# Column sums of squares taken tile by tile on TensorE in two norms beside the first attention

## What is computed

```python
def rms_norm(x, g):
    xf = x.astype(jnp.float32)
    y = xf * lax.rsqrt(jnp.mean(xf * xf, axis=-1, keepdims=True) + EPS)
    return (y * g.astype(jnp.float32)).astype(x.dtype)

a = spatial_gating_unit(jax.nn.gelu(u), jax.nn.gelu(v), ...)      # 512 tokens x 512
b = nsa_attention(q, kv, gl, ...)                                 # the first attention
mixed = jnp.concatenate([rms_norm(a, mix_out_g[l, 0]), rms_norm(b, mix_out_g[l, 1])], axis=-1)
x = x + mixed @ w_out[l]
...
k, v = jnp.split(rms_norm(mem, kv_norm_g) @ w_mkv, 2, axis=-1)    # 256 tokens x 1024
```

## Time and profile before

| | |
|---|---|
| median of 3 runs | 2616.11 us (2615.8 to 2616.41) |
| the profiled execution, its own time | 2613.08 us |
| its span, first to last instruction | 2611.3 us |
| mean granted clock of PE | 0.968 of 2.4 GHz |
| PE busy | 2467.3 us, 94% of the span |
| POOL busy | 532.1 us, 20% |
| the loop of the first attention | about 208 to 376 us |

### The profile page before, as it was taken

How to read it: one execution, slowest core, us unless ns; L and a number is a source line. 1 busy time by engine, 2 the same in 40 slices (tenths; PEclk the granted TensorE clock), 3 DMA queues, 4 the chain that set the end, 5 groups by cost and what they waited for, 6 DMA issues and landing times.

```text
span 2611.3 us, 34190 instructions
## 1 busy us (share of the span) xinstructions
PE 2467.3 (94%) x14039; PEld 1976.7 (76%) x14039; DVE 1180.7 (45%) x1849; ACT 915.4 (35%) x1576; POOL 532.1 (20%) x381
## 2 busy tenths in 40 slices
PE   6887888899999999999999999999989999999998
PEld 5665666677788876778877888888866677878876
DVE  3735545454433444562257313323457633733432
ACT  3324543342222234552246211123335533632223
POOL 3003222140200211231004110012433210321023
PEclk8987899999999989999999999999989999999998
DMA  5231133245443311001210122113121023023232
GB/s 166 65 115 33 33 119 124 74 153 162 142 133 97 109 59 41 25 17 49 81 41 2 49 73 65 57 57 106 50 85 33 25 65 113 9 65 111 75 109 85
DMA packets 195740, 200.60 MB, mean 77 GB/s; under 512 B 15832, under 2 KB 189624, under 8 KB 195330
## 3 DMA queue, kind: packets, MB, share of 16 engines
q1 hardware_dynamic: 191106, 178.23, 21.8%
q10 hardware_dynamic: 4480, 20.19, 2.0%
HBM read 187.92 MB, written 10.49 MB: 76 GB/s over the span
## 4 chain that ended last, share of the span: by engine, by line
PE 85%; DVE 6%; ACT 4%; POOL 2%; issue 2%; DMA 1%; ACTq 0%; POOLq 0%; SPq 0%; DVEq 0%
PE PS L719 20%; PE PS L720 20%; PE PS L722 20%; PE PS L837 5%; PE PS L867 4%; PE PS L851 3%; DVE WL L1888 1%; PE PS L798 1%; ACT WH L1317 1%; PE PS L910 1%; PE PS L937 1%; PE PS L923 1%; PE PS L966 1%; POOL RB L2638 1%; PE PS L775 1%
## 5 line engine op out<-in xcount | busy, mean ns | idle before, releaser
L719 PE MATMUL PS<-HH,WH 128*128 128x512 f32 (+3 forms) x2048 | 757.0, 370 | 9.7 <-DVE WL L1888 4.8
L720 PE MATMUL PS<-HL,WH 128*128 128x512 f32 (+3 forms) x2048 | 726.9, 367 | 0.0
L722 PE MATMUL PS<-HH,WL 128*128 128x512 f32 (+3 forms) x2048 | 659.2, 365 | 0.0
L1888 DVE TENSOR_TENSOR WL<-WB,WH 128x2048 fp32r<-128x2048 f32 (+3 forms) x158 | 324.0, 2051 | 666.4 <-ACT WH L1317 658.5
L719 PEld LDWEIGHTS PS<-HH,WH 128*128 128x128 f32 (+1 forms) x2048 | 384.1, 188 | 117.0 <-issue 13.9
L720 PEld LDWEIGHTS PS<-HL,WH 128*128 128x128 f32 (+1 forms) x2048 | 384.0, 187 | 71.6 <-issue 2.9
L1317 ACT ACTIVATE WH<-WB 128x2048 fp32r<-128x2048 f32 (+3 forms) x158 | 265.1, 1678 | 340.1 <-PE PS L722 270.7
L722 PEld LDWEIGHTS PS<-HH,WL 128*128 128x128 f32 (+1 forms) x2048 | 348.1, 188 | 44.6
L2663 POOL TENSOR_SCALAR SA<-SA,ST 128x768 f32<-128x768 f32 (+4 forms) x80 | 142.0, 1776 | 534.8 <-DVE ST L1969 534.8
L2638 POOL TENSOR_TENSOR RB<-RB,SA 128x512 f32<-128x512 f32 (+2 forms) x65 | 89.3, 1374 | 391.2 <-ACT SA L1336 330.0
L1957 DVE TENSOR_REDUCE ST<-PS 128x1 f32<-128x768 f32 (+4 forms) x176 | 130.0, 739 | 71.0 <-PE PS L837 57.5
(11 more groups left out here) (366 smaller groups left out, 3716.7 us busy)
## 6 DMA issues: line engine op xcount, KB each, us to landing
WB<-in_w_in_dram SPq DMA_DIRECT2D x61, 1024.0 KB, 5.2
WB<-in_w_ff_dram SPq DMA_DIRECT2D x32, 1024.0 KB, 5.4
WB<-in_w_mod_dram SPq DMA_DIRECT2D x24, 1024.0 KB, 5.3
WB<-in_w_branch_dram SPq DMA_DIRECT2D x24, 512.0 KB, 3.5
WB<-in_w_o_dram SPq DMA_DIRECT2D x8, 1024.0 KB, 5.2
WB<-in_w_in_dram SPq DMA_DIRECT2D x14, 512.0 KB, 5.1
XTc<-xd ACTq DMA_DIRECT2D x2, 3072.0 KB, 10.0
WB<-in_cmp_w_dram SPq DMA_DIRECT2D x4, 1024.0 KB, 5.4
```

The lines of the kernel that those rows point to most:

```text
L719: pe.matmul(D[0:m, d + o:d + o + w], h, xh[:, o:o + w], start=first, stop=False)
L720: pe.matmul(D[0:m, d + o:d + o + w], h, xl[:, o:o + w], start=False, stop=False)
L722: t = pe.matmul(D[0:m, d + o:d + o + w], lo, xh[:, o:o + w], start=False, stop=last)
L1888: dve.tensor_tensor(b.of(WL[s % NH]), b.of(WB[b.n % NW]), b.of(WH[s % NH]).bitcast(F32), ALU.subtract).then_inc(*done("wl", s))
```

## The change

On PE, `paced_norm` no longer calls `sum_columns`. From its third item on it waits for the squares of one tile in each item and sums that tile at once with `add_columns`, the first tile opening the sum and the last closing it. On POOL the adds are gone, their items are empty. On ACT the squares go to the same buffers, which come free when PE has summed them. Sum, root, reciprocal and spread keep their items, except that the last sum stands one item ahead of where `sum_columns` stood.

```diff
             def paced_norm(N, nf, n):            # PE
-                for f in range(nf):
-                    yield
                 yield
                 yield
-                yield from paced_columns(N, nf, n, ("hn", N, nf - 1))
+                D = slot(("norm", N), ("hn", N, nf - 1))
+                for f in range(nf):
+                    pe.wait_ge(*at("sq", N, f))
+                    add_columns(D, 0, n, SA[sa[N, f]] if f else RB[rb[N]], f == 0, f == nf - 1).then_inc(
+                        *(done("nsum", N) if f == nf - 1 else done("ncol", N, f)))
+                    yield
+                yield
+                yield
+                spread_columns(N, n)
+                yield
...
             def paced_norm(N, nf, n, size, src, ready, dst):            # ACT
                 for f in range(nf):
-                    sq(N, f, src(f), ready(f), ("nsum", N))
+                    sq(N, f, src(f), ready(f), ("ncol", N, 0), added=("ncol", N, f) if f < nf - 1 else ("nsum", N))
...
             def paced_norm(N, nf, n, lo, hi):            # POOL
-                for f in range(nf):
-                    if f:
-                        add_sq(N, f, n)
-                    yield
-                for _ in range(5):
+                for _ in range(nf + 5):
                     yield
```

More of the change, by code:

```diff
@@ L1322, in begin, with sq @@
                     split_hi(s)
-            def sq(N, f, src, ready, freed=None, k1=128, last=None):
+            def sq(N, f, src, ready, freed=None, k1=128, last=None, added=None):
                 n = src.shape[-1]
@@ L1330, in sq @@
                     D = taken(rb, RB, N, freed)
+                elif added is not None:
+                    D = taken(sa, SA, (N, f), added)
                 elif f == last:
```

## The result

The changed kernel takes 2623.98 us in the median of 6 runs (2619.68 to 2626.2), the kernel before 2616.15 us in 6 runs beside it (2615.57 to 2616.58). The ratio is 1.003, 95% interval 1.002 to 1.004: slower by 7.8 us, 0.3%. A second series on another chip gave 1.0041 (1.0027 to 1.0056), 10.9 us by the medians (2625.95 against 2615.10). My forecast was 2619.4 with a range of 2613.5 to 2624.5. The time lies inside, near its upper end, and it is the first rival's: the clock stayed low.

What follows compares the result with a forecast made beforehand. PE, busy for 94% of the span, was taken to bound the kernel. `am` +1.0 and `mn` +2.3 gave +3.3 us on the median of 2616.11, so 2619.4 us; range 2613.5 to 2624.5.

Steps and rivals of the forecast that it cites:

- the first rival: Slower: PE stays at 0.50 from 247 to beyond 274 us, nothing given back; some +7 us, 2623; chance 0.21.
- POOL's relief: Both norms: removing ten POOL adds saves PE 3.25 us of waits in `am` and 1.63 in `mn`, 4.9 us.
- `am`: +2.4 us at the spread: `am` norm: three more sums 5.2 us, new wait 0.5, less 3.25 of waiting for POOL: spread 2.4 us later.
- the new wait: `am` norm: PE waits for ACT's squares of tile 0 before the third pair's scores, costing 0.5 us.
- what I let come back: `am`: work sliding behind the clock rise at 223.15 runs in half the time, leaving +1.0 us of +2.4.
- the rise fails: `mn` norm: one-column sums act as idle time, PE's clock stays low at 254.0, spread 5.4 us later.
- The later series: Later in the profile before: PE 100% busy with one-column sums only, yet its clock falls from 0.99 to 0.50.
- The sign that I gave: `mn` norm, what would show the forecast right: the spread starts between 264 and 268 us from the span's start.
- What is given back: Behind the `mn` sums: few waits, clock rises sooner; half of 5.4 us returned or never lost, leaving +2.3.
- The rivals of the other side: Faster: sums count as work for the clock, which rises in `am` near 217 and stays up; -5.5 us, 2610.6; chance 0.07.
- Elsewhere: Outside the two norms: DVE's and ACT's order stays, nothing behind 376 us changes in order; no term in the sum.

Runs made afterwards that it cites:

- the run with the sums together: Against the kernel before, only `am` changed: POOL's adds gone, all four one-column tile sums placed where the one sum stood; 2618.2 us, ratio 1.0007.
- wide sums: Changed kernel with the same matmuls in both norms, each moving 128 columns of ones instead of one; 2617.9 us, repeated 2618.0 us.
- the eight wide records: Kernel before, POOL adding as ever, with the single sums of `am` and `mn` (4 and 2 matmuls) moving 128 columns; 2616.7 us, ratio 1.0.

## Why the prediction was right, and where it was off

**What bounds the kernel, and POOL's relief.** Right. The 3.25 us were worth 3.05 us at the `am` spread, and the relief as a whole 3.8 us at the `mn` spread, where I had 4.9.

**`am`: +2.4 us at the spread.** Right: 2.16. The price of a record at the low clock (0.215 us) and the new wait (0.5 us) are both in the timeline, and the run with the sums together confirms the wait. Wrong is what I let come back, from 2.4 down to 1.0. With `am` changed alone the shift is 3.4 us at the last narrow scores, not 1.0, and 4.9 by the medians. I had the clock rise at 223.15 as before, 15 us behind the first scores; it rose at 226.0, 19 us behind them, with the sums together too (18.8), and 8.2 us behind them with wide sums. The one-column sums in front of it are the reason that I had myself given for `mn` and had not applied here. That term was mis-sized by more than 2 us.

**`mn`: sums at the low clock, the rise fails.** Right, and for the reason given: the low stretch runs from 250.0 to 270.3, the shift from spread to spread is 5.5 us, where the working at the low clock had 5.4. The later series was the right row to decide by. The wide sums, which take about as long, and the eight wide records in the kernel before show that the width of the sums made the difference. The sign that I gave was missed all the same: the `mn` spread started at 269.2, not between 264 and 268: there the shifts of both norms stand in full, 2.2 and 5.5 us.

**What is given back.** This is the step that failed. I took half of the 5.4 us as returned between 262 and 274 us (half would leave 2.7; the sum had 2.3), since PE would have few waits there and rise sooner. It did rise once, at 270.3, for 3.4 us, and fell again until 280.4; what came back was 0.7 us (62.15 less 54.47 is 7.7, and 7.0 at the last scores). The price of the first rival, +7, is what was measured, and its condition (the rise at 254.0 fails and none comes before 274.5) was met but for that short stretch; read strictly it was not met. I had given it 0.21 because I hoped for the clock on no row at all: the 13.6 us at 0.50 with 12.17 us busy spoke against it. That the time fell inside the range at all is in part luck: the forecast was 4.6 us too low, and in the second series the changed kernel came out 10.9 us slower, where my range ended at +8.4.

**The rivals of the other side.** That sums keep the clock up is refuted for one-column sums (0.50 from 250.0 to 270.3 us). With wide ones PE was granted 1.00 from 232.0 to 259.5 us, yet the kernel did not come near the 2610.6 of that rival (2617.9). The sentence of the Trainium skill ("TensorE: Matmul & The Clock Gate", Part 1, "What's actually happening") that activity releases the throttle holds only if activity isn't read as PE busy: 20.30 us busy of 20.30 at 0.50 above.

**Elsewhere.** That behind 376 us nothing is changed was right for the order, not for one execution's time: the two profiles differ by 9.5 us in span, of which 7.0 lie in the attention. The rest moves by some 3 us in either direction from execution to execution. The kernel before shows by itself that single executions differ by more than that (2611.4 to 2620.7).

## What to carry to other kernels

A reduction over partitions by matmuls with one column costs PE a weight load each, and here PE stayed at 0.50 while it did them, busy for 20.30 of 20.30 us. Where PE bounds the kernel, such sums should be few. Wide ones were the lesser evil when they had to be many (2618 against 2624 to 2626 us), but still no faster than one sum (2615.7). Taking work from an idle engine to the one that bounds is a gain only if the wait removed is longer than the work at the clock that is granted there: here 3.25 us of waiting against 5.2 us of sums. A third engine may be the better place for it: DVE did the same adds in about half of POOL's time each, and PE waited 1.65 us for them where it had waited 3.25 behind POOL's.

## What the runs showed of the hardware that was not expected

At the low clock eight records of 128 columns took little more than eight of one column (1.92 and 1.84 us). At the high clock the difference was larger: 0.64 us against 0.54 for four records, from start to start. The kernel was 6 to 8 us faster with the wider ones all the same, since PE was granted 1.00 where the narrow ones left it at 0.50. With only eight records made wide, the clock rose 12.0 us behind the first scores in place of 15.3. And a faster clock by itself brought nothing where PE next waited for others: the kernel with one wide sum was granted 0.95 for 3.4 us, where before it was 0.50, and took the same time.
